# Two more early groups and paired 64-column value products in a two-layer encoder kernel

## The reference

```
for l in range(2):
    h = x @ w_in[l]                       # Fourier input, q, k, v, two gates
    q, k = rope(rms_norm(q)), rope(rms_norm(k))      # 8 query heads, 2 key/value heads, 64 wide
    y_a = softmax(q k^T / 8) v  -> @ w_branch_attn   # query heads 0-3 use kv head 0, 4-7 kv head 1
    x = layer_norm(alpha * x + (gate_f * y_f + gate_a * y_a) @ w_out)
    # retrieval over 128*128 single-neuron experts, 8 retrieval heads, best 16 of each
    s1, s2 = (x @ w_query) . sub_keys     # two sets of 128 scores per head
    eidx, gate = top16 of the sums of the two top16s, softmax
    y = sum over chosen experts: gate * gelu(u[e] . x) * v[e]
    x = layer_norm(alpha * x + y)
```

## Time and profile before

| | us |
|---|---|
| median of 3 runs (lowest, highest) | 3995.9 (3995.53, 3997.57) |
| profiled execution, its time | 3997.35 |
| its span, first to last instruction | 3995.6 |
| mean granted TensorE clock | 0.983 of 2.4 GHz |
| PE busy | 3807.2 (95%) |
| DVE busy | 2760.0 (69%) |
| POOL busy | 2505.9 (63%) |
| ACT busy | 753.7 (19%) |

### The profile page before, as it was taken

The page is one execution under the profiler, slowest core; times in us unless marked ns, Lnnn a source line. Parts: engine busy times, 40 slices in busy tenths (PEclk is TensorE's granted clock), DMA queues, the critical chain, the costliest instruction groups (busy, mean ns, idle before and its releaser), DMA issues.

```text
span 3995.6 us, 54149 instructions
## 1 busy us (share of the span) xinstructions
PE 3807.2 (95%) x19024; PEld 3144.7 (79%) x19024; DVE 2760.0 (69%) x3953; ACT 753.7 (19%) x1305; POOL 2505.9 (63%) x1268
## 2 busy tenths in 40 slices
PE   6999996999999999999989999889999999999998
PEld 5778885778878888888877798667788788888886
DVE  7545999996998444444584559999789974444445
ACT  1551112331111111010115401133311110111101
POOL 5435574447777676766654455844577777667674
PEclk9999998999999999999999999999999999999999
DMA  3112234776554333333221123357764543333331
GB/s 143 53 64 93 93 137 140 230 221 235 188 189 158 125 128 116 115 126 120 90 86 64 72 90 111 127 164 220 235 225 178 199 143 121 116 126 126 115 115 74
DMA packets 224634, 546.56 MB, mean 137 GB/s; under 512 B 9728, under 2 KB 141056, under 8 KB 174976
## 3 DMA queue, kind: packets, MB, share of 16 engines
q1 hardware_dynamic: 46656, 335.57, 23.3%
q10 hardware_dynamic: 177856, 209.36, 16.1%
HBM read 442.12 MB, written 102.76 MB: 136 GB/s over the span
## 4 chain that ended last, share of the span: by engine, by line
PE 61%; DVE 30%; issue 6%; DVEq 1%; POOL 1%; ACT 1%; DMA 0%; ACTq 0%; SPq 0%; POOLq 0%
PE bank L1087 19%; PE bank L1089 19%; PE bank L1088 19%; DVE hot L988 3%; DVE Wl L1020 3%; DVE hot2l L993 2%; DVE hot L989 2%; DVE ki L908 2%; DVE Wf L1016 1%; PE bank L1210 1%; DVE pick L951 1%; DVE kv__78 L905 1%; DVE X L1037 1%; DVE pos L908 1%; DVE pick L948 1%
## 5 line engine op out<-in xcount | busy, mean ns | idle before, releaser
L383 POOL TENSOR_TENSOR part_l<-landing,part_h 128x1024 fp32r<-128x1024 f32 x632 | 1705.6, 2699 | 52.8
L380 POOL TENSOR_SCALAR part_h<-landing 128x1024 fp32r<-128x1024 f32 x632 | 810.3, 1282 | 1402.8 <-PE bank L1089 764.1
L1087 PE MATMUL bank<-XTh,part_h 128*128 128x512 f32 (+1 forms) x2688 | 1054.1, 392 | 11.1 <-DVE XTl L711 7.7
L1088 PE MATMUL bank<-XTl,part_h 128*128 128x512 f32 (+1 forms) x2688 | 1038.7, 386 | 0.0
L1089 PE MATMUL bank<-XTh,part_l 128*128 128x512 f32 (+1 forms) x2688 | 1038.4, 386 | 0.0
L1087 PE MATMUL bank<-part_h,Wh 128*128 128x512 f32 x2048 | 800.5, 391 | 9.9 <-DVE X L1037 7.1
L1089 PE MATMUL bank<-part_h,Wl 128*128 128x512 f32 x2048 | 797.3, 389 | 0.0
L1088 PE MATMUL bank<-part_l,Wh 128*128 128x512 f32 x2048 | 797.0, 389 | 0.0
L1087 PEld LDWEIGHTS bank<-XTh,part_h 128*128 128x128 f32 x2688 | 509.6, 190 | 110.0 <-POOL part_l L383 4.4
L1089 PEld LDWEIGHTS bank<-XTh,part_l 128*128 128x128 f32 x2688 | 508.6, 189 | 102.6
L1088 PEld LDWEIGHTS bank<-XTl,part_h 128*128 128x128 f32 x2688 | 509.6, 190 | 97.1 <-issue 0.5
(11 more groups left out here) (165 smaller groups left out, 3542.3 us busy)
## 6 DMA issues: line engine op xcount, KB each, us to landing
landing<-stream SPq DMA_DIRECT2D x316, 1024.0 KB, 4.8
dense_gates<-spill ACTq DMA_DIRECT2D x32, 2048.0 KB, 9.4
gate<-dense_gates ACTq DMA_DIRECT2D x64, 1024.0 KB, 4.8
early_acts<-early ACTq DMA_DIRECT2D x128, 256.0 KB, 2.3
acts_in<-early_acts ACTq DMA_DIRECT2D x32, 1024.0 KB, 7.5
LNP<-ln ACTq DMA_DIRECT2D x5, 1024.0 KB, 4.7
X<-x SPq DMA_DIRECT2D x4, 512.0 KB, 9.7
keyT<-keys ACTq DMA_DIRECT2D x2, 1024.0 KB, 4.8
```

Of the source, the lines that this page charges most:

```text
L380: nc.gpsimd.tensor_scalar(part_h[k][:, w], landing[s][:, w], 1.0, 0.0, ALU.mult, ALU.add).then_inc(high_part, 1)
L383: nc.gpsimd.tensor_tensor(part_l[k][:, w], landing[s][:, w], part_h[k][:, w].bitcast(F32), ALU.subtract).then_inc(split.sem, 1)
L1087: nc.tensor.matmul(dst, sth, mvh, start=first, stop=False)
L1088: nc.tensor.matmul(dst, sth, mvl, start=False, stop=False)
```

## The change

Two independent edits. First, `EG` goes from 16 to 18 and `E_BEFORE` from 12 to 16: four more u pieces are multiplied before the routing turn, groups 16 and 17 become early groups, and 14 late groups are left. Second, the order of heads becomes 0, 4, 1, 5, 2, 6, 3, 7; `PT` becomes three buffers, each of one head; and `values` is called once per pair of heads, with 64 stationary columns for each head, the two heads' products alternating and going to the lower and upper 64 rows of one PSUM bank. `o_copy` and `o_rest` then work on 128 rows, four times in a layer instead of eight. `oTl` moves in memory.

```diff
-EG = 16
-E_BEFORE, E_AFTER = 12, 4
+EG = 18
+E_BEFORE, E_AFTER = 16, 4
...
-        PT = overlay("PT", 58, [P, 2, TB, S])
+        PT = [overlay(f"PT{i}", kib, [P, TB, S]) for i, kib in enumerate((58, 66, 24))]
...
                 def p_copy(u):
-                    h, tb = u // TB, u % TB
+                    n, tb = u // TB, u % TB
                     act.wait_ge(p_turned.sem, p_turned.at(l, u + 1))
-                    if h >= 2:
-                        act.wait_ge(pv_done.sem, pv_done.at(l, h - 1))
+                    if n == 2:
+                        act.wait_ge(y_low.sem, y_low.at(l, GROUPS))
+                    if n >= 3:
+                        act.wait_ge(pv_done.sem, pv_done.at(l, (n - 3) // 2 + 1))
...
-                def o_copy(h):
-                    g, j = h // PAIRS, h % PAIRS
-                    act.wait_ge(pv_done.sem, pv_done.at(l, h + 1))
-                    nc.scalar.copy(oTh[g * HD:(g + 1) * HD, j, :],
-                                   bank[4 + h % 2][g * HD:(g + 1) * HD, :]).then_inc(o_high.sem, 1)
+                def o_copy(j):
+                    act.wait_ge(pv_done.sem, pv_done.at(l, j + 1))
+                    nc.scalar.copy(oTh[:, j, :], bank[4 + j % 2][:]).then_inc(o_high.sem, 1)
...
-                def values(h):
-                    pe.wait_ge(p_copied.sem, p_copied.at(l, TB * (h + 1)))
-                    if h >= 2:
-                        pe.wait_ge(o_low.sem, o_low.at(l, h - 1))
+                def values(j):
+
+                    pe.wait_ge(p_copied.sem, p_copied.at(l, 2 * TB * (j + 1)))
+                    if j >= 2:
+                        pe.wait_ge(o_low.sem, o_low.at(l, j - 1))
                     for s in range(TB):
-                        ins = nc.tensor.matmul(bank[4 + h % 2][:], qkv[:, s, NORMED * HD:QKV], PT[:, h % 2, s, :],
-                                               start=(s == 0), stop=(s == TB - 1))
+                        for g in range(KV_HEADS):
+                            v = slice((NORMED + g) * HD, (NORMED + g + 1) * HD)
+                            ins = nc.tensor.matmul(bank[4 + j % 2][g * HD:(g + 1) * HD, :], qkv[:, s, v],
+                                                   PT[(2 * j + g) % 3][:, s, :], start=(s == 0), stop=(s == TB - 1))
...
-                    if u % TB == 1 and u > TB:
-                        values(u // TB - 1)
+                    if u % (2 * TB) == 1 and u > 2 * TB:
+                        values(u // (2 * TB) - 1)
```

More of the change, by code:

```diff
@@ L148, in build @@
         oTh = overlay("oTh", 44, [P, PAIRS, S], F32R)
-        oTl = overlay("oTl", 24, [P, PAIRS, S], F32R)
+        oTl = overlay("oTl", 16, [P, PAIRS, S], F32R)
         xfT = overlay("xfT", 16, [P, GROUPS, S])
@@ L247, in build @@
         p_copied = tally("p_copied", 0, 32)
-        pv_done = tally("pv_done", 0, HEADS)
-        o_high = tally("o_high", 0, HEADS)
-        o_low = tally("o_low", 0, HEADS)
+        pv_done = tally("pv_done", 0, PAIRS)
+        o_high = tally("o_high", 0, PAIRS)
+        o_low = tally("o_low", 0, PAIRS)
         gatef = tally("gatef", 0, KD)
@@ L471, in p_copy @@
                 def p_copy(u):
-                    h, tb = u // TB, u % TB
+                    n, tb = u // TB, u % TB
                     act.wait_ge(p_turned.sem, p_turned.at(l, u + 1))
-                    if h >= 2:
-                        act.wait_ge(pv_done.sem, pv_done.at(l, h - 1))
-                    nc.scalar.copy(PT[:, h % 2, :, tb * P:(tb + 1) * P],
-                                   bank[2 + u % 2][:].rearrange("p (s t) -> p s t", s=TB)).then_inc(p_copied.sem, 1)
-                def o_copy(h):
-                    g, j = h // PAIRS, h % PAIRS
-                    act.wait_ge(pv_done.sem, pv_done.at(l, h + 1))
-                    nc.scalar.copy(oTh[g * HD:(g + 1) * HD, j, :],
-                                   bank[4 + h % 2][g * HD:(g + 1) * HD, :]).then_inc(o_high.sem, 1)
+                    if n == 2:
+                        act.wait_ge(y_low.sem, y_low.at(l, GROUPS))
+                    if n >= 3:
+                        act.wait_ge(pv_done.sem, pv_done.at(l, (n - 3) // 2 + 1))
+                    nc.scalar.copy(PT[n % 3][:, :, tb * P:(tb + 1) * P],
+                                   bank[2 + u % 2][:].rearrange("p (s t) -> p s t", s=TB)).then_inc(p_copied.sem, 1)
+                def o_copy(j):
+                    act.wait_ge(pv_done.sem, pv_done.at(l, j + 1))
+                    nc.scalar.copy(oTh[:, j, :], bank[4 + j % 2][:]).then_inc(o_high.sem, 1)
                 fill_gates(-1)
@@ L498, in _ @@
                         nc.scalar.copy(yTh[:, g, :], yf[:, g, :]).then_inc(y_high.sem, 1)
-                    if u % TB == 2 and u > TB:
-                        o_copy(u // TB - 1)
+                    if u % (2 * TB) == 2 and u > 2 * TB:
+                        o_copy(u // (2 * TB) - 1)
                 p_copy(31)
-                o_copy(HEADS - 1)
+                o_copy(PAIRS - 1)
                 fill_gates(31)
@@ L821, in row_max, with o_rest @@
                                             ALU.mult).then_inc(max_ready.sem, 1)
[L823 to L827, removed]
+                def o_rest(j):
+                    dve.wait_ge(o_high.sem, o_high.at(l, j + 1))
+                    nc.vector.tensor_tensor(oTl[:, j, :], bank[4 + j % 2][:], oTh[:, j, :].bitcast(F32),
                                             ALU.subtract).then_inc(o_low.sem, 1)
@@ L854, in _ @@
                                                 ALU.subtract).then_inc(y_low.sem, 1)
-                    if u % TB == 3 and u > TB:
-                        o_rest(u // TB - 1)
-                o_rest(HEADS - 1)
+                    if u % (2 * TB) == 3 and u > 2 * TB:
+                        o_rest(u // (2 * TB) - 1)
+                o_rest(PAIRS - 1)
                 fill_products(31)
@@ L1186, in scores @@
                 def scores(u):
-                    h, tb = u // TB, u % TB
+                    h, tb = u // TB % KV_HEADS * PAIRS + u // TB // KV_HEADS, u % TB
                     q, g = stacked(h)[:, tb * P:(tb + 1) * P], h // PAIRS
@@ L1272, in _ @@
                     turn_probs(u)
-                    if u % TB == 1 and u > TB:
-                        values(u // TB - 1)
+                    if u % (2 * TB) == 1 and u > 2 * TB:
+                        values(u // (2 * TB) - 1)
                 for _ in range(FILL_TURNED):
                     next(fill)
-                values(HEADS - 1)
+                values(PAIRS - 1)
                 for _ in range(FILL_VALUES):
@@ L1283, in _ @@
                 pe.wait_ge(p_copied.sem, p_copied.at(l, 32))
-                pe.wait_ge(o_low.sem, o_low.at(l, HEADS))
+                pe.wait_ge(o_low.sem, o_low.at(l, PAIRS))
                 for m in range(KD):
```

## The result

The changed kernel runs in 3928.2 us (median of 4 runs, 3926.7 to 3930.5) against 3996.7 us for the kernel before on the same chip: a ratio of 0.983 with a 95% interval of 0.9814 to 0.9845, 68.5 us less. A repetition in a later set of runs gave 3927.6 us. The forecast was 3927.5 us.

The account below looks back on a forecast made before the run. PE bounds attention and late groups, DVE paces the dense gates, and PE waits 26.7 us at the turn. Early pieces 47.2 plus values 21.2 give 68.4 us less: 3927.5 us, range 3917 to 3953.

Parts of the forecast that it names:

- The hole: Routing turn: PE's 26.7 us wait for DVE's tables filled; turn near 636, dense gates 18.7 us later per layer.
- POOL's supply: Before the turn: POOL, at 12.2 us a piece against PE's 10.87, makes PE wait about 2.1 us once.
- DVE under POOL: Last two lookup rounds before the turn: POOL beside them makes DVE's tables 4.4 us later, at 632.5, costing nothing.
- The warm clock: Routing turn: PE coming straight from work runs the 12 transposes faster, 0.2 us gained on DVE's path.
- What is given back: Two groups turn from late (43.52 us) to early (22.36 us): 42.3 us less per layer, net 23.6.
- The value products: Attention: two heads' products overlap, 9 steps instead of 16, 4.2 us a call, 10.6 us gained per layer.
- B: Rival: the two value tiles run one after the other, only the early part counts, 3948.7 us; chance 0.25.
- C: Rival: value products one by one with weight loads exposed, 24.3 us on top, 3973 us; chance 0.03.
- D: Rival: the hole can't be filled, turn at 670.4, only the values' gain remains, 3974.7 us; chance 0.06.
- E: Rival: alternating tiles serialise PE wholly, 782 ns per value instruction instead of 430, 3994 us; chance 0.04.

Follow-up runs that it names:

- fourteen pieces: Changed kernel with fourteen early pieces before the turn and six after the dense gates: 3948.5 us, 21.0 us slower than sixteen where 12 were expected.
- exchanged loops: Changed kernel with the two value-product loops exchanged, all products of the first head, then all of the second: 3944.1 us, ratio 0.9864.
- the run in groups of four: Changed kernel with value products alternating in groups of four instructions per head (two blocks of one head, two of the other): 3929.3 us, ratio 0.9830.

## Why the prediction was right

**The hole.** PE was to lose its wait of 26.7 us at the turn and did. The turn was to come at 636 us in the changed kernel, and came at 636.05. That is closer than the terms: what stands ahead of DVE's last conversion became 11.4 us shorter, not 10.6, and the turn came 19.3 us later after it, not 18.9. Counted from DVE's last conversion before the lookup (552.96 and 541.60 us) the end of DVE's wait, the first `wtl`, moved from 77.2 to 96.7 us, so the dense gates start 19.6 us later; the sum had 18.7. The two rows of that conversion, kernel before and kernel after:

```profile
552.96 1.55 DVE L940 CAST kf<-ki 128x1024 f32<-128x1024 uint32 x1
```

```profile
541.60 1.54 DVE L938 CAST kf<-ki 128x1024 f32<-128x1024 uint32 x1
```

**POOL's supply.** The forecast was one wait of 2.1 us; it was 0.3 and 1.7 us. The halves became ready in the pattern read off before the turn: POOL's starts in the changed kernel, six half pieces in 36.8 us, 6.1 us each:

```profile
569.64 3.10 POOL L380 TENSOR_SCALAR part_h<-landing 128x1024 fp32r<-128x1024 f32 x1
...
606.47 3.10 POOL L380 TENSOR_SCALAR part_h<-landing 128x1024 fp32r<-128x1024 f32 x1
...
622.95 1.09 POOL L380 TENSOR_SCALAR part_h<-landing 128x1024 fp32r<-128x1024 f32 x1
...
626.61 1.09 POOL L380 TENSOR_SCALAR part_h<-landing 128x1024 fp32r<-128x1024 f32 x1
```

The last two rows show what the pattern left out. It is the pace beside DVE's lookups; they end at 619.57 us, and from then on a half piece takes POOL 3.7 us. The slowing goes both ways.

**DVE under POOL.** This step failed in size. The tables were to be 4.4 us later; they end at 626.78, 85.2 us after the conversion instead of 75.7, so 9.5 us later. The end of the lookups accounts for 4.5 us of it, as expected; the rest is the four short products behind them, 5.80 us instead of 0.90. It cost nothing here, since the turn came another 9 us later; with fourteen pieces, where the tables set the turn, it is part of the miss.

**The warm clock.** I gave 0.2 us for faster transposes. They are 1.35 us faster and it gained nothing: ACT's first copy begins 1.21 us after the turn, where it was 0.94 us, since a gelu and the issue of its store now stand just before it. ACT in the kernel after:

```profile
636.25 0.60 ACT L543 ACTIVATE early<-bank 128x512 f32<-128x512 f32 x1 [4.85 <-PE bank L1087]
636.88 0.34 ACTq L545 DMA_DIRECT2D early_acts<-early  x1
637.26 0.48 ACT L571 COPY routeT<-bank 128x384 f32<-128x384 f32 x1 [0.42 <-PE bank L1390]
```

This and 0.4 us by which PE arrived later make the 0.9 us between 18.7 and 19.6.

**What is given back.** 22.36 and 43.52 us per group held. The early edit was to gain 23.6 us per layer; alone it gained 22.1, and with the 19.6 instead of 18.7 it is 22.7. What is left, 0.6 us, is less than the scatter of the dense gates named above, 265.2 to 267.9 us.

**The value products.** The mechanism was the chosen one; the size was low. I put a call at 4.2 us, it takes 3.79, 3.06 us gained per pair and 12.3 per layer where 10.6 were forecast. The term that was off is the number of steps: I assumed nine for the order A A B B; it is eight, because the first product of the second head begins with the first of the first head, not with its second. That gain arrives in full: from the first unit's transposes to the start of the last call PE takes 280.39 - 141.01 = 139.4 us before and 268.91 - 142.13 = 126.8 us after, 12.6 us less, for seven calls of 3.42 us that became three of 3.79. The rows of the last calls, before and after:

```profile
280.39 3.59 PE L1210 MATMUL bank<-PT,qkv 128*128 128x512 f32 x8
```

```profile
268.91 3.65 PE L1211 MATMUL bank<-PT,qkv 128*64 128x512 f32 x16
```

The two misses, 1 to 1.5 us per layer too much for the early edit and 1.7 too little for the values, nearly cancel. That the total is 68.5 against 68.4 us is luck.

**The rivals.** B (one after the other) would have shown 6.9 us a call; with exchanged loops, where most neighbours share a half, a call took 5.53. C (exposed weight loads) is out: the loads of 137 ns pair up inside the steps. The Trainium skill (TensorE: Matmul & The Clock Gate, The mechanism) lists that weight loads overlap running matmuls only when the row group differs. That doesn't hold for these tiles, which share all rows. The same section of the Trainium skill also lets a load for a background weight buffer go ahead, which no run here can tell apart. Nor, if the counts of starts are read rightly, does the strict order of starts hold that this section of the Trainium skill states: the second head's first instruction is third in the program and two start together at 175.5 us. The "up to 2x" of the Trainium skill for 64 columns (TensorEngine Tiling (Array Packing), Theoretical Speedup) fits: 6.85 / 3.79 = 1.8. D would have needed POOL at 17.3 us a piece; it stayed at 12.3. E would have needed 782 ns a step; it is 430 for two.

## What to carry to other kernels

A wait on another engine can be filled with work that is brought forward, and what that earns is the length of the hole, not the length of the work: four pieces beyond it cost 43.5 us per layer here and gave 42.3 back. Before filling, check the supplier of the filling work: it must be ahead by as much as it is slower, and here it slowed the engine that was waited for. Where a product uses half of the array's columns, two such products for different halves of the output rows, near each other in PE's order, took the time of one here.

## What the runs showed of the hardware

- Two plain float32 products of 64 stationary columns, 128 rows and 512 moving columns, to the lower and the upper 64 rows of one PSUM bank, run at the same time: sixteen instructions in eight steps of 0.43 us, the step of one instruction of a 128-column product. A burst of sixteen costs 3.79 us with its entry and exit.
- PE seems to start an instruction for the other half past up to three waiting instructions of the first half. This is inferred from the counts of simultaneous starts and from the 3.63 us of the run in groups of four. With eight in a row it still overlapped four.
- A short two-input DVE instruction (128 x 128, 285 ns) beside POOL's splits took up to 2485 ns, about one POOL instruction (2.39 to 2.51 us); four in a row took 5.80 us instead of 0.90. The Trainium skill (GPSIMD Engine Reference, Key points) states that the two engines contend when a DVE instruction has two SBUF inputs; the size for a short instruction is what these rows add. In turn a half piece takes POOL 6.1 us beside DVE's lookups and 3.7 us after them.

```profile
L963 DVE TENSOR_TENSOR route<-route,gsum x8: 278/1632/2485, 621.0 to 2569.4; 128x128 f32<-128x128 f32 x8
```
